# Wide input products in the two Hyena layers: high weights against both parts of the rows at once

## What is computed

```python
p = xn @ w_in + b_in                       # 1024 -> 3072
pp = jnp.pad(p, ((0, 0), (r, r), (0, 0)))
p = conv_b + sum(pp[:, j:j + L] * conv_w[j] for j in range(HY_SHORT))   # 3 taps
x1, x2, v = jnp.split(p, 3, axis=-1)
kf = jnp.fft.rfft(hyena_filters(L, ...), axis=0)   # filters divided by their sum of absolute values
for o, gate in enumerate((x1, x2)):
    z = gate * (long_conv(z, kf[:, o]) + fbias[o] * z)
return z @ w_out + b_out
```

## Time and profile before

| | |
|---|---|
| median of three runs | 2899.77 us |
| the profiled execution's own time | 2904.63 us |
| its span, first to last instruction | 2902.8 us |
| TensorE busy | 2854.7 us (98%) |
| VectorE busy | 2094.6 us (72%) |
| ScalarE busy | 1686.4 us (58%) |
| mean granted TensorE clock | 0.996 |

### The profile page before, as it was taken

The page is one execution under the profiler, slowest core; times in us unless marked ns, Lnnn a source line. Parts: engine busy times, 40 slices in busy tenths (PEclk is TensorE's granted clock), DMA queues, the critical chain, the costliest instruction groups (busy, mean ns, idle before and its releaser), DMA issues.

```text
span 2902.8 us, 41709 instructions
## 1 busy us (share of the span) xinstructions
PE 2854.7 (98%) x17504; PEld 2519.1 (87%) x17504; DVE 2094.6 (72%) x1937; ACT 1686.4 (58%) x1713; POOL 432.1 (15%) x279
## 2 busy tenths in 40 slices
PE   8999999999999999999999999999999999999999
PEld 8999988999988888888888796888898888796888
DVE  6787676678768888888888685665666576675664
ACT  6446554545657767767767562554855465362552
POOL 1130331113010000000000002231023133002230
PEclk9999999999999999999999999999999999999999
DMA  7444555544449989889989741455455656540553
GB/s 240 158 133 160 183 183 187 189 146 146 160 158 370 352 342 373 347 342 376 348 334 380 249 131 44 147 190 193 153 160 185 197 159 194 196 146 29 160 185 120
DMA packets 359711, 612.93 MB, mean 211 GB/s; under 512 B 11519, under 2 KB 323925, under 8 KB 324576
## 3 DMA queue, kind: packets, MB, share of 16 engines
q1 hardware_dynamic: 355936, 597.99, 59.1%
q10 hardware_dynamic: 3104, 12.10, 1.2%
q0 software_dynamic: 480, 0.12, 0.0%
HBM read 608.99 MB, written 1.05 MB: 210 GB/s over the span
## 4 chain that ended last, share of the span: by engine, by line
PE 96%; DVE 2%; ACT 1%; DMA 1%; issue 0%; POOL 0%; ACTq 0%; SPq 0%; DVEq 0%; POOLq 0%
PE ps L370 21%; PE ps L371 11%; PE ps L357 8%; PE ps L359 8%; PE ps L358 8%; PE ps L1363 5%; PE ps L1365 5%; PE ps L1364 5%; PE ps L1341 3%; PE ps L1339 3%; PE ps L1340 3%; PE ps L1904 2%; PE ps L739 2%; PE ps L1919 2%; PE ps L1413 1%; PE ps L1872 1%
## 5 line engine op out<-in xcount | busy, mean ns | idle before, releaser
L284 DVE TENSOR_TENSOR wlo<-raw,whi 128x2048 fp32r<-128x2048 f32 (+2 forms) x574 | 1326.1, 2316 | 317.9 <-ACT whi L273 299.2
L273 ACT ACTIVATE whi<-raw 128x2048 fp32r<-128x2048 f32 (+2 forms) x574 | 1085.4, 1893 | 244.6 <-PE ps L371 113.5
L370 PE MATMUL ps<-HXB,whi 128*128 128x512 f32 x1760 | 619.2, 397 | 2.7 <-DVE HXB L498 2.7
L357 PE MATMUL ps<-HX,whi 128*128 128x256 f32 x1808 | 521.1, 288 | 17.1 <-DVE wlo L284 12.3
L358 PE MATMUL ps<-HX,whi 128*128 128x256 f32 x1808 | 512.2, 283 | 0.0
L359 PE MATMUL ps<-HX,wlo 128*128 128x256 f32 x1808 | 512.2, 283 | 0.0
L371 PE MATMUL ps<-HXB,wlo 128*128 128x256 f32 x1760 | 490.9, 279 | 0.0
L370 PEld LDWEIGHTS ps<-HXB,whi 128*128 128x128 f32 x1760 | 330.3, 188 | 83.8 <-DVE HXB L498 3.9
L357 PEld LDWEIGHTS ps<-HX,whi 128*128 128x128 f32 x1808 | 347.5, 192 | 23.4 <-ACT HX L574 10.6
L358 PEld LDWEIGHTS ps<-HX,whi 128*128 128x128 f32 x1808 | 347.7, 192 | 3.4 <-issue 3.3
L359 PEld LDWEIGHTS ps<-HX,wlo 128*128 128x128 f32 x1808 | 347.5, 192 | 0.0
(11 more groups left out here) (338 smaller groups left out, 3978.1 us busy)
## 6 DMA issues: line engine op xcount, KB each, us to landing
raw<-in_c_experts SPq DMA_DIRECT2D x264, 1024.0 KB, 4.8
raw<-in_w_in SPq DMA_DIRECT2D x71, 1024.0 KB, 5.1
raw<-in_ff_w_gate SPq DMA_DIRECT2D x44, 1024.0 KB, 5.4
raw<-in_ff_w_up SPq DMA_DIRECT2D x44, 1024.0 KB, 5.3
raw<-in_ff_w_down SPq DMA_DIRECT2D x32, 1024.0 KB, 4.9
raw<-in_dense_w SPq DMA_DIRECT2D x30, 1024.0 KB, 5.3
raw<-in_hy_w_in SPq DMA_DIRECT2D x24, 1024.0 KB, 5.0
raw<-in_ff_w_down SPq DMA_DIRECT2D x16, 768.0 KB, 4.2
```

The lines of the kernel that those rows point to most:

```text
L273: e.activation(m.whi[:, i % NSPLIT, 0:n], m.raw[:, i % NRAW, 0:n], ACT.Copy).then_inc(*k.up("act", "hi", i))
L284: e.tensor_tensor(m.wlo[:, i % NRAW, 0:n], m.raw[:, i % NRAW, 0:n], hi, ALU.subtract).then_inc(*k.up("dve", "lo", i))
L357: e.matmul(o, wh, xh, start=first and t == k0, stop=False)
L370: e.matmul(o[:, :], wh, x[:, :, kx + t, :], start=first and t == k0, stop=False)
```

## The change

The input products of both Hyena layers use the wide form. ScalarE writes only the low half, with the bias, into the padded rows. VectorE adds the high half to both rows in one instruction of 512 elements, placed at the head of its turn, and this instruction frees the two banks. ScalarE waits for it before it multiplies the first tap.

```diff
@@ pe_hyena
-        pe_gemm(e, k, m, s, "in", m.HX, [j], fresh=None if j else ("hx", last))
+        pe_wide_gemm(e, k, m, s, "in", m.HX, j, fresh=None if j else ("hx", last))
@@ act_hyena
         e.wait_ge(*k.at("g", s, "in", j))
-        o = ps(k, m, "g", s, "in", j)
+        low = pair_halves(k, m, "g", s, "in", j)[1]
         for i in range(2):
             c = 2 * j + i
             if c >= PADS:
                 e.wait_ge(*k.at("cv", s, c - PADS))
-            e.activation(pp[c][:, 1:L + 1], o[:, i * L:(i + 1) * L], ACT.Identity, bias=m.col("hy_b_in_2", 24 * f + c)).then_inc(
-                *k.up("act", "pp", s, c))
-        k.note("act", "free", "g", s, "in", j)
+            e.activation(pp[c][:, 1:L + 1], low[:, i, :], ACT.Identity, bias=m.col("hy_b_in_2", 24 * f + c)).then_inc(
+                *k.up("act", "low pp", s, c))
         e.wait_ge(*k.at("pads", s))
-        e.wait_ge(*k.own("act"))
+        e.wait_ge(*k.at("pp", s, j))
@@ dve_hyena
     for j in range(12):
+        e.wait_ge(*k.at("low pp", s, 2 * j + 1))
+        both = pad_rows(m)[:, 2 * j % PADS:2 * j % PADS + 2, 1:L + 1]
+        e.tensor_tensor(both, both, pair_halves(k, m, "g", s, "in", j)[0], ALU.add).then_inc(*k.up("dve", "free", "g", s, "in", j))
+        k.note("dve", "pp", s, j)
         dve_panel(e, k, m, panels)
```

More of the change, by code:

```diff
@@ L1805, with pad_rows @@
 FILTER_TURNS = {0: ("spec", 0, 3), 3: ("l1", 0), 4: ("spec", 1, 0), 5: ("spec", 1, 1), 6: ("spec", 1, 2), 7: ("spec", 1, 3), 10: ("l1", 1)}
+def pad_rows(m):
+    return m.buf(0)[:, 0:PADS * (L + 2)].rearrange("p (t n) -> p t n", t=PADS)
 def pads(m):
-    rows = m.buf(0)[:, 0:PADS * (L + 2)].rearrange("p (t n) -> p t n", t=PADS)
-    return [rows[:, c % PADS, :] for c in range(24)]
+    return [pad_rows(m)[:, c % PADS, :] for c in range(24)]
 def dft_view(m):
```

## The result

The change makes the kernel slower: 2931.58 us (median of four runs, 2929.94 to 2939.86) against 2900.78 us (four runs, 2898.01 to 2903.72). The ratio is 1.0108, with an interval from 1.0094 to 1.0121. The profiled execution took 2931.57 us (span 2929.8, mean granted clock 0.990), 26.9 us more than the profiled one of before.

A forecast was written before the change was run, and what follows sets the result against it. TensorE, holding 96% of the chain, was taken as the bound. Full-clock terms of +16.9 us plus clock terms of 8.4, 1.0 and 0.8 gave +27.1, against the median 2899.77 about 2927 us, range 2914 to 2935.

The forecast's parts named there:

- chains to l1, four: Turn 0's end to the one-column sums, twice per layer: 22.05 us instead of 18.99, 4 x 3.06 = 12.2 us later.
- tails: Last products to second turning of rows: 6.09 us instead of 3.74, 2.35 more, 4.7 in both layers.
- bank wait in hy1: First wide product of hy1 starts 2.5 us later, as VectorE must free a spec group's bank; none in hy0.
- gain of the wide form that is left: Six panels per layer outside the stretches to l1, 0.21 us saved each: 2.5 us in all.
- clock behind the four l1: Granted clock falls behind each new l1 wait of about 3.7 us: 4 x 2.1 = 8.4 us, bounds 0 and 10.
- clock in the tails: Existing falls at the tails cost more with longer idleness: 0 to 0.9 us each, 0.5 taken, together 1.0.
- clock behind the bank wait: Possible clock fall behind the 2.5 us wait at hy1's first product: 0 to 2.5 us, 0.8 taken.
- Rival 2: VectorE is not late at l1, its list runs past itself: +2.2 us at full clock, 2902.0 us; chance 0.05.
- rival 3: Only the wide pace matters, tail and bank wait hidden as well: -5.0 us, 2894.8 us; chance 0.04.
- The bound of 2.5: Upper bound in us for one clock fall behind l1, from an earlier half-clock stretch with 4.92 us busy.
- Rival 1: Same waits, but the clock stays up at most of them: +16.9 us, 2916.7 us; chance 0.17.

The follow-up runs named there:

- narrow_wait: Kernel before, narrow products, with only VectorE waiting at the head of each turn until ScalarE has written both padded rows: 2917.6 us, ratio 1.0045.
- wide_reordered: Changed kernel with the addition right ahead of VectorE's taps, ScalarE's taps, last low part and second l1 later, one bank skipped: 2903.92 us, ratio 1.0006.
- low_first: Changed kernel with VectorE making the low part of a panel ahead of the addition instead of behind it: 2919.54 us, ratio 1.0064.
- bank_skip: Changed kernel with one bank left out before the spec pieces of hy1, so its first pair avoids a spec group's bank: 2928.58 us, ratio 1.0081.
- no_add: Changed kernel without the addition and its waits, ScalarE freeing the banks, output lacking the high halves: 2899.87 us, ratio 0.9983.
- kept_busy: Changed kernel with 26 matmuls of 256 columns, result overwritten, ahead of each of the four l1 waits: 2922.27 us, ratio 1.0054.
- wide_again: The changed kernel once more, unaltered, against the kernel before: 2935.15 us, ratio 1.0117.
- narrow_wait_busy: Kernel before with VectorE waiting for ScalarE's padded rows at each turn's head, plus 8 matmuls of 256 columns ahead of each l1: 2916.81 us, ratio 1.0051.
- tail_busy: Kernel before with 20 matmuls of 256 columns at the second turning, behind TensorE's wait for VectorE: 2907.69 us, ratio 1.0017.
- tail_busy_ahead: Kernel before with 20 matmuls of 256 columns at the second turning, ahead of TensorE's wait for VectorE: 2900.57 us, ratio 0.9995.
- narrow_fill: Kernel before with the second l1 moved from turn 10 to between the two turnings of rows: 2899.24 us, ratio 0.9989.

## Why the prediction was right

The time was forecast at 2927 and the range held it: 2931.58. The terms, in us, against the ledger:

| term | forecast | measured |
|---|---|---|
| chains to l1, four | +12.2 | +12.2 |
| tails | +4.7 | +4.4 |
| bank wait in hy1 | +2.5 | +2.2 |
| gain of the wide form that is left | -2.5 | -1.9 |
| clock behind the four l1 | +8.4 | +12.4 |
| clock in the tails | +1.0 | about 0 |
| clock behind the bank wait | +0.8 | +1.9 |
| elsewhere | 0 | -4.2 |
| sum | +27.1 | +27.0 |

- **The chain** was right in its instructions and its length: 22.05 us worked out, 22.05 measured. The waits it makes are 3.2 to 3.5 us and not 3.7, as TensorE's own products were slower than taken (below). L1883's operand ends at 1696.86 + 1.22 = 1698.08, and l1 starts at 1698.23. narrow_wait shows that the place of a wait does it, without new work, and wide_reordered that the same work in another place costs next to nothing. Rival 2, that VectorE is not late, is refuted by the four waits of the change itself; wide_reordered has the kind of order that it would have needed.
- **The tail** was right; low_first takes part of it away by the one instruction that was named.
- **The bank** was right as a wait, 2.17 us for 2.5; bank_skip takes it away.
- **The gain** of the wide form was read from one stretch. Over 19 tiles of turns 1 and 2 of hy0 the distance is (1686.01 - 1679.30) / 19 = 0.3532 us per tile, not 0.3467, so a panel gains 0.11 us there instead of 0.21. No_add has 4.3 us for all 24 panels, near the 5.0 of the prediction, and 0.3 once its bank wait is taken off. Its ratio (-0.17%, interval -0.30 to -0.03%) looks like rival 3's -5.0, but its profile puts some 3 us of it to clock falls that are missing in the tails, so that would be luck.
- **The step that was mis-sized** is the clock behind l1. I took 2.1 us each, between 1.6 and 2.5, from the lengths of the two falls of before. The fall behind l1 lasts longer, 6.4 us at 0.50 with TensorE busy all the time, and costs 3.0 to 3.2: l1 to the next start is 10.43 to 10.62 us where kept_busy and low_first have 7.41 to 7.55 without a fall. The bound of 2.5 came from a stretch of 6.40 us in which only 4.92 were busy; here 6.40 of 6.40 are, and half of that is 3.2. With three falls gone and one shorter, the four stretches behind l1 are 10.5 us shorter in kept_busy, and its whole execution 9.3. Rival 1 is refuted: the clock fell behind all four. The tails' +1.0 was too much: from the second turning to the next layer's first product the change differs from before by +0.14 and -0.02 us.
- **The total** agrees in part by luck. Profile to profile, the stage lost 31.2 us instead of 27.1, and the two executions happen to differ by -4.2 elsewhere, in code that the change doesn't touch. Ahead of the stage it is -2.1, about half of it around 850 us and the rest around 1640 us, beside stretches at 0.50 that both executions have (the later one lasts 3.4 us instead of 6.8). In two feed-forward layers further on the wide products took their quicker pace and gave back 6.7. Three clock falls that the profiled execution of before doesn't have cost 4.4. The medians, 30.8 us apart, agree with the 31.2 of the stage. The profiled execution of before was 3.9 us above its median of four runs, that of after was at its own.

## What to carry to other kernels

An engine that looks half idle has spare time only where its list lets it: when an edit puts a wait for this turn's products at the head of a list, add up everything that is queued behind it to the next instruction on which the bottleneck waits, and place the wait behind whatever does not need it. A cheaper product form (here 4.3 us in 24 panels) is worth less than one such wait with its clock fall (6.1 us). And price a wait of TensorE with its clock fall: behind l1 the waits of 3.2 us cost about 3.1 us more, and those of 1.05 us cost 1.6 to 3.1 us more. Where the fall comes and how long it lasts can differ from one execution to the next, so forecast it as a range, and read a difference of a few us between two profiles by where their falls lie.

## What was not expected of the hardware

**Two paces of the same products.** A tile of one 512- and one 256-column matmul takes one of two times, and keeps it through a stretch. In the same last feed-forward layer, 23 tiles apart, of the kernel before and then of the one after:

```profile
2759.78 0.40 PE L370 MATMUL ps<-HXB,whi 128*128 128x512 f32 x1
...
2767.92 0.40 PE L370 MATMUL ps<-HXB,whi 128*128 128x512 f32 x1
```

```profile
2759.92 0.39 PE L370 MATMUL ps<-HXB,whi 128*128 128x512 f32 x1
...
2767.89 0.40 PE L370 MATMUL ps<-HXB,whi 128*128 128x512 f32 x1
```

That is 0.3539 and 0.3465 us per tile, both at full clock, for the same instructions. It doesn't take two kernels: these are the same tiles of the changed kernel in its first profile and in wide_again:

```profile
2479.33 0.39 PE L370 MATMUL ps<-HID,whi 128*128 128x512 f32 x1
...
2487.30 0.40 PE L370 MATMUL ps<-HID,whi 128*128 128x512 f32 x1
```

```profile
2482.21 0.40 PE L370 MATMUL ps<-HID,whi 128*128 128x512 f32 x1
...
2490.33 0.40 PE L370 MATMUL ps<-HID,whi 128*128 128x512 f32 x1
```

That is 7.97 and 8.12 us for 23 tiles. The narrow tile was 0.3598 wherever it was looked at. What chooses the pace wasn't found. Against the narrow tile the wide form saves 6 or 13 ns. By the Trainium skill ("TensorE: Matmul & The Clock Gate", Part 1, "Wait — 56ns, not 53.3ns?"), which the prediction weighed, it would be an estimated 2.5 ns, and its formula has a single pace. The measurements differ from both, and they decide.

**The clock.** Counted over the thirteen traces, the granted clock went to 0.50 at or behind these places (up to 4 us from their start) so often:

| place | wait of TensorE, us | falls |
|---|---|---|
| l1 in the change, wide_again, bank_skip | 3.2 to 3.5 | 12 of 12 |
| l1 in low_first | 2.83; 1.31; 1.01 twice | 1; 1; 1 of 2 |
| l1 in narrow_wait | 1.05 | 4 of 4 |
| l1 in wide_reordered | 0.69; none three times | 1; 1 of 3 |
| l1 in narrow_wait_busy | none, filled | 3 of 4 |
| l1 in kept_busy | 0.33 or none, filled | 1 of 4 |
| l1 in before, no_add, tail_busy, tail_busy_ahead, narrow_fill | none | 0 of 20 |
| second turning in before; in no_add | 2.6 | 2 of 2; 0 of 2 |
| first product of the next layer, all traces | 2.12 | 14 of 26 |

The last place stands in code that no run edited. The prediction took from the earlier trace rows that the clock stays up there; in the change it fell, and the stretch behind it took 1.5 us longer:

```profile
1833.56 0.36 PE L357 MATMUL ps<-HX,whi 128*128 128x256 f32 x1 [2.12 <-ACT HX L539]
```

```profile
1835.20:1838.40 3.20, 3.20 (x17) 3.20 (x16) 0.56 (x2) 0.44 (x1) 0.00 (x0) 0.50 0.00 0
```

So the waits of 2.8 us and more ahead of l1 had a fall in 13 of 13 cases, and of the shorter ones the same wait at the same place had one in some cases and none in others. In and near the stage the stretches at 0.50 last about 3.4 or about 6.8 us. Neither the length of the pause nor its presence separates the cases, and what does stays open.
